# Attention of a hybrid layer taken step by step between the quarters of w_in's blocks

## The chip, the cores and the metric

One core of one Trainium2 chip runs the whole kernel. The metric is the device time of one execution in microseconds (us). The engines are named PE (TensorE), DVE (VectorE), ACT (ScalarE), POOL (GpSimd) and SP (SyncE, which here only issues DMAs).

## What is computed

One inference step of a two-layer backbone (DEPTH 2) for two groups of 128 tokens (g = 0 and 1), each 1024 wide, all in float32. A layer does, for h = the adaLN-modulated input:

```
gate_b, gate_c, u, q, k, v, g_conv, g_attn = split(h @ w_in)              # 1024 x 6656
y_conv = (gate_b * short_conv(gate_c * u)) @ w_conv_out
s1, s2 = q1 @ k1^T, q2 @ k2^T      (two halves of 64 of each of 8 heads)
p      = softmax(s1 / 8) - lam * softmax(s2 / 8)
o      = rms_norm(p @ v) * (1 - lam_init);  y_attn = o @ w_attn_out
x      = layer_norm(ALPHA * x + gate * ((sigmoid(g_conv) * y_conv + sigmoid(g_attn) * y_attn) @ w_out))
```

Group 1 has rotary positions on q and k, and 128 more cached keys and values. Behind it each layer has a channel mixer: a dense SwiGLU in layer 0, the top 2 of 8 SwiGLU experts in layer 1. The adaLN vectors are silu(c) @ ada_w, 24 blocks of 512 columns for both layers. Keys and values are outputs too.

## The kernel before

**Products in three passes.** A float32 weight block (1024 x 512 or 512 x 1024, 2 MB) is split into `w_hi` (ACT, `hi`, L535) and `w_lo` = raw - w_hi (DVE, `lo`, L816; a few blocks by POOL, `rests`, L441). PE multiplies with `mm3` (L1270 to L1272): hi*hi, lo*hi, hi*lo. A block is handled in four quarters (`PARTS`); `w_hi` and `w_lo` hold one buffer for each quarter, so the split of quarter t + 4 waits until PE has multiplied quarter t (`parts_free`). A quarter is 12 matmuls of 512 columns.

**Loads.** SP loads blocks into `raw`, a ring of three slots (`SLOTS`) of two halves each, in an order written out by hand. A half is 1 MB. A slot's half is loaded again once the block three places before it in `stream` is used up. The ada blocks stand in three lumps: 4 at the start, 12 behind `w_attn_out`'s first block of layer 0, 8 at the same place of layer 1 (`ADA_AT`).

**Order of a layer's first part.** 13 blocks of w_in (q, k, v, then gate_b, gate_c, u, then the four blocks of gates), whose results turn through three pairs of PSUM banks; the convolution's transposes (L1512) stand between the last of them. Then `w_conv_out`. Then attention: 16 heads (`JOBS`, 8 of group 0 and of group 1), in 20 steps of a software pipeline over PE, ACT and DVE. In step n, PE transposes q and k of head n (L1557 to L1560), multiplies the scores of head n - 1 (L1570) into one of two pairs of banks, takes ada halves (`ada_half`, L1465: 4 small products, 8 records in the trace; one half in each of 16 steps, and 8 more behind them in layer 0), transposes the probabilities of head n - 3 (L1583) and multiplies head n - 4 with v (L1591). DVE takes the maxima (L1176, L1178), scales and subtracts the two softmaxes (L1183 to L1187) and copies; ACT copies q and k (L734), takes exponentials with their sums (L742) and squares (L751). `ada_copy` (L578) empties the ada bank after each four blocks, `ada_turn` (L1476) transposes it. Behind attention come the transposes of the normed heads (L1533), `w_attn_out`, the gates' broadcast (L1360), `w_out` and the layer norm.

Each engine runs its program strictly in the order of its text, and waits on semaphores. POOL makes the normed x of the layer from `xhat` (`make_x`, L456 and L457), which lies where v's blocks will be written, so v's evacuation waits for it (`x_ok`).

Of the kernel before, what the change touches and what calls it, by code (L numbers as in the profile page):

```python
# [57 lines left out]
def program(nc, a, out):  # L58
    with ExitStack() as ctx:
# [37 lines left out]
        rsum = sb("rsum", [P, 2, 2])  # L97
# [21 lines left out]
        cv = sb("cv", [P, G, T])  # L119
        bank = [ctx.enter_context(nc.psum_tensor(f"bank{i}", [P, COL], F32)) for i in range(8)]  # L120
# [15 lines left out]
        att = flat[:, 0:2048]  # L136
# [3 lines left out]
        qkT = flat[:, 2048:2048 + 6 * T].rearrange("p (b k) -> p b k", b=2)  # L140
# [3 lines left out]
        rope_t = flat[:, 12288:13312]  # L144
# [15 lines left out]
        def s_bank(j, i):  # L160

            return bank[j % 2 + 6 * i]
# [7 lines left out]
        def head(b0, j):  # L170
# [31 lines left out]
            sem(n) for n in ("j_qk", "j_qkT", "j_s", "j_max", "j_exp", "j_p", "j_pT", "j_pTc", "j_o", "j_oc", "j_sq"))  # L202
        osd_ok, on_ok, oT_t, oT_hi, oT_ok = (sem(n) for n in ("osd_ok", "on_ok", "oT_t", "oT_hi", "oT_ok"))
# [22 lines left out]
        ADA_AT = [(0, 4), (IN_BLOCKS + 2, 12), (turn0[1] * SLOTS + IN_BLOCKS + 2, 8)]  # L226
        N_FIXED = (turn0[1] + Q_LAYER) * SLOTS
        stream = []
        for d in range(N_FIXED):
            for at, n in ADA_AT:  # L230
                if at == d:
                    stream += [("ada", sum(kind == "ada" for kind, _ in stream) + i) for i in range(n)]
            stream.append(("weights", d))
# [3 lines left out]
        def ring(q, s):  # L237

            if isinstance(q, int) and q * SLOTS + s < N_FIXED:
                i = place["weights", q * SLOTS + s]  # L240
                return i % SLOTS, i // SLOTS + 1
            return s, q + (RAW0 + 1)
# [10 lines left out]
        RUNS_IN = IN_BLOCKS // SLOTS  # L253
        RUNS_QKV = (B_GCONV - B_Q) // SLOTS
        ORDER_IN = list(range(B_Q, B_GCONV)) + list(range(B_GB, B_Q)) + list(range(B_GCONV, IN_BLOCKS))


        def halves(l, step):
            first = QUAD * 2 * (1 if l == 0 else 4)
            if step < JOBS:  # L260
                return [first + step]
            if l == 0:
                return [first + JOBS + 2 * (step - JOBS) + i for i in range(2)]
            return []

        TURN_AT = {9: 0, 17: 1}

        def quad_of(l, i):
            return i + (1 if l == 0 else 4)
# [9 lines left out]
        def _(sp):  # L279
            def free(i, half):  # L280

                if i >= SLOTS:
                    kind, n = stream[i - SLOTS]
                    if kind == "ada":
                        sp.wait_ge(ada_sum, n + 1)
                    else:
                        sp.wait_ge(lo_done, PARTS * n + 2 * half + 2)

            def load(q, s, half, shape, src):
                if isinstance(q, int) and q * SLOTS + s < N_FIXED:  # L290
                    free(place["weights", q * SLOTS + s], half)
                else:

                    sp.wait_ge(lo_done, (q - 1) * (PARTS * SLOTS) + (PARTS * s + 2 * half + 2))
                fill(ring(q, s)[0], half, shape, src)

            def fill(r, half, shape, src):
                n = shape[0] * shape[1]
                dst = raw[:, r, 2 * half * UNIT:2 * half * UNIT + n].rearrange("p (k n) -> p k n", n=shape[1])
                sp.dma_start(dst, src).then_inc(raw_in[r][half], 16)  # L300

            def conditioning(first, n):
                for k in range(first, first + n):
                    i, c0 = place["ada", k], k % ADA_BLOCKS * COL
                    for half in range(2):
                        free(i, half)
                        fill(i % SLOTS, half, (4, COL), a["ada_w"][k // ADA_BLOCKS][half * 4 * P:(half + 1) * 4 * P, :]
                             .rearrange("(k p) n -> p k n", p=P)[:, :, c0:c0 + COL])

            def columns(q, s, w, c0, n):  # L310

                for half in range(2):
                    load(q, s, half, (4, n), w[half * 4 * P:(half + 1) * 4 * P, :]
                         .rearrange("(k p) n -> p k n", p=P)[:, :, bass.ds(c0, n)])

            def rows(q, s, w, k0, k1):

                for half in range(2):
                    load(q, s, half, (k1 - k0, COL), w[k0 * P:k1 * P, half * COL:(half + 1) * COL]
                         .rearrange("(k p) n -> p k n", p=P))  # L320

            def expert(q, wg, wu, wd, others=None):
                for j in range(PER_EXPERT):
                    if others is not None and j == SLOTS:
                        others()
                    if j < 2 * CHUNKS:
                        columns(q + j // SLOTS, j % SLOTS, (wg, wu)[j % 2], j // 2 * COL, WIDE[j // 2])
                    else:
                        rows(q + j // SLOTS, j % SLOTS, wd, *DOWN[j - 2 * CHUNKS])
# [10 lines left out]
            conditioning(0, 4)  # L340
            for l in range(DEPTH):
                for pos, b in enumerate(ORDER_IN):
                    columns(turn0[l] + pos // SLOTS, pos % SLOTS, a["w_in"][l], b * COL, COL)
                q = turn0[l] + RUNS_IN
                rows(q, 1, a["w_conv_out"][l], 0, 4)
                rows(q, 2, a["w_attn_out"][l], 0, 4)
                conditioning(*((4, 12), (16, 8))[l])
                rows(q + 1, 0, a["w_attn_out"][l], 4, 8)
                rows(q + 1, 1, a["w_out"][l], 0, 4)
                rows(q + 1, 2, a["w_out"][l], 4, 8)  # L350
                q += 2
                if l == 0:
                    for e in range(DENSE_PARTS):
                        expert(q + e * Q_EXPERT, a["ffn_w_gate"][0][:, e * FF:(e + 1) * FF],
                               a["ffn_w_up"][0][:, e * FF:(e + 1) * FF], a["ffn_w_down"][0][e * FF:(e + 1) * FF, :])
                else:
                    def of(e):
                        return (a[n][0, bass.ds(e, 1)].rearrange("e d f -> (e d) f")
                                for n in ("moe_w_gate", "moe_w_up", "moe_w_down"))

                    def first_rows():
                        sp.wait_ge(x_sent, 16 * 2 * G)
                        x_load(0)
                        sp.wait_ge(gx_t, 1)
                        x_load(1)

                    def one(p, e):
                        def between():
                            y_store(p - 1, y_sent)
                            sp.wait_ge(gx_t, p + 1)  # L370
# [1326 lines left out]
```

## Time and profile before

| | |
|---|---|
| median of 3 runs | 1261.44 us (1261.29 to 1262.12) |
| the profiled execution | 1262.02 us, span 1260.2 us, mean granted clock 0.962 |
| w_in's blocks, layer 0 and 1 (from the first product) | 146.2 us and 157.2 us (with conv_out in layer 1) |
| attention, layer 0 and 1 | 63.7 us and 52.1 us |

The span is from the first to the last instruction. Busy time of PE counts matmuls whose ends are modelled: in a dense stretch they overlap, so that distances are better taken from start to start. The stretch from 44.7 to 190.9 us is w_in's 13 blocks of layer 0, 201.7 to 265.4 us its attention; 525.1 to 682.3 us is w_in and conv_out of layer 1, and 682.3 to 734.4 us its attention.

### The profile page before, as it was taken

The page shows a single profiled execution, that of the slowest core. Times are in us where ns is not written, and L with a number is a line of the kernel's source. Part 1 is how long each engine was busy: PE and PEld are TensorE (multiplying, and loading weights), DVE is VectorE, ACT ScalarE, POOL GpSimd, SP SyncE. Part 2 cuts the span into 40 slices and gives each one's busy share as a digit, 9 for nine tenths or more (in the row PEclk, how much of TensorE's full clock was granted, in tenths as well). Part 3 has the DMA queues.
Part 4 walks back from the last instruction along what each step waited for, and adds up shares of the span by engine and source line. Part 5 has one row for each costly group of instructions (what it writes and reads, how often), then busy time and mean ns, then how long its engine had stood idle before and what let it go on. Part 6 is the DMA issues. An engine that isn't in the chain of part 4 may idle for free.

```text
span 1260.2 us, 15915 instructions
## 1 busy us (share of the span) xinstructions
PE 1143.3 (91%) x5645; PEld 918.6 (73%) x5645; DVE 856.0 (68%) x1227; ACT 712.9 (57%) x1018; POOL 150.0 (12%) x140
## 2 busy tenths in 40 slices
PE   5699999889999999899999989649999999999980
PEld 1588885468789889788886478538888788788870
DVE  1574686635675455585676846539889889889965
ACT  1444455534644444444445644438888888888862
POOL 5040003000360000440003000340000000000001
PEclk9799999999999999999999989869999999999995
DMA  9777657985359746565656964069999999999952
GB/s 333 281 262 231 198 172 265 386 325 192 96 171 413 270 155 210 141 225 189 223 169 229 387 215 134 1 239 337 372 381 385 381 374 383 378 385 381 374 211 100
DMA packets 165849, 332.57 MB, mean 264 GB/s; under 512 B 6528, under 2 KB 27120, under 8 KB 165792
## 3 DMA queue, kind: packets, MB, share of 16 engines
q1 hardware_dynamic: 158288, 307.78, 69.6%
q0 software_dynamic: 7472, 24.03, 5.5%
q8 instruction: 36, 0.59, 0.2%
q14 instruction: 21, 0.17, 0.0%
q10 hardware_dynamic: 32, 0.01, 0.0%
HBM read 314.48 MB, written 17.30 MB: 263 GB/s over the span
## 4 chain that ended last, share of the span: by engine, by line
PE 79%; DVE 7%; DMA 5%; ACT 4%; issue 3%; POOL 0%; SPq 0%; ACTq 0%; DVEq 0%; POOLq 0%
PE bank L1270 24%; PE bank L1272 23%; PE bank L1271 23%; DMA raw<-in_ada_w 4%; PE bank L1465 2%; ACT w_hi L535 2%; PE bank L1360 1%; DVE xT_lo L851 1%; PE bank L1420 1%; DVE x L864 1%; DVE w_lo L816 1%; ACT xT_hi L558 1%; PE bank L1570 1%; PE bank L1409 1%; DVE st L821 1%
## 5 line engine op out<-in xcount | busy, mean ns | idle before, releaser
L816 DVE TENSOR_TENSOR w_lo<-raw,w_hi 128x1024 fp32r<-128x1024 f32 (+1 forms) x484 | 568.4, 1206 | 225.5 <-ACT w_hi L535 223.6
L535 ACT ACTIVATE w_hi<-raw 128x1024 fp32r<-128x1024 f32 (+1 forms) x504 | 500.2, 1008 | 360.4 <-PE bank L1272 360.1
L1270 PE MATMUL bank<-w_hi,xT_hi 128*128 128x512 f32 (+1 forms) x1056 | 407.9, 386 | 18.5 <-DVE w_lo L816 12.3
L1272 PE MATMUL bank<-w_lo,xT_hi 128*128 128x512 f32 (+1 forms) x1056 | 402.9, 382 | 0.0
L1271 PE MATMUL bank<-w_hi,xT_lo 128*128 128x512 f32 (+1 forms) x1056 | 402.7, 381 | 0.0
L1270 PEld LDWEIGHTS bank<-w_hi,xT_hi 128*128 128x128 f32 x1056 | 199.6, 189 | 60.1 <-issue 11.6
L1272 PEld LDWEIGHTS bank<-w_lo,xT_hi 128*128 128x128 f32 x1056 | 199.4, 189 | 35.0
L1271 PEld LDWEIGHTS bank<-w_hi,xT_lo 128*128 128x128 f32 x1056 | 199.7, 189 | 33.0
L1270 PE MATMUL bank<-w_hi,hT_hi 128*128 128x512 f32 x360 | 142.9, 397 | 3.7 <-issue 3.7
L1272 PE MATMUL bank<-w_lo,hT_hi 128*128 128x512 f32 x360 | 141.5, 393 | 0.0
L1271 PE MATMUL bank<-w_hi,hT_lo 128*128 128x512 f32 x360 | 141.3, 392 | 0.0
L441 POOL TENSOR_TENSOR w_lo<-raw,w_hi 128x1024 fp32r<-128x1024 f32 x20 | 50.7, 2555 | 404.0 <-ACT w_hi L535 404.0
L1270 PEld LDWEIGHTS bank<-w_hi,hT_hi 128*128 128x128 f32 x360 | 68.3, 190 | 17.5 <-issue 4.1
L1272 PEld LDWEIGHTS bank<-w_lo,hT_hi 128*128 128x128 f32 x360 | 68.1, 189 | 14.6
L1271 PEld LDWEIGHTS bank<-w_hi,hT_lo 128*128 128x128 f32 x360 | 68.4, 190 | 13.6
L1465 PE MATMUL bank<-raw,cond_st 128*32 128x512 f32 x384 | 57.0, 671 | 18.3 <-DMA raw<-in_ada_w 13.8
L506 POOL DMA_INDIRECT work<-y_rows,row_no x4 | 3.9, 968 | 389.9 <-DMA y_rows<-work 389.0
L1465 PEld LDWEIGHTS bank<-raw,cond_st 128*32 128x32 f32 x384 | 8.0, 113 | 40.6 <-DMA raw<-in_ada_w 27.9
L742 ACT ACTIVATE work<-bank,nmx 128x128 f32<-128x128 f32 (+1 forms) x64 | 26.4, 418 | 13.1 <-DVE nmx L1178 12.7
L751 ACT ACTIVATE cv<-work 128x128 f32<-128x128 f32 x32 | 9.9, 310 | 30.6 <-DVE work L1199 30.6
L456 POOL TENSOR_TENSOR x<-work 128x1024 f32<-128x1024 f32 x8 | 21.7, 2710 | 33.7 <-DVE work L910 26.6
L457 POOL TENSOR_TENSOR x<-x,work 128x1024 f32<-128x1024 f32 x8 | 24.3, 3035 | 0.6
(235 smaller groups left out, 886.4 us busy)
## 6 DMA issues: line engine op xcount, KB each, us to landing
raw<-in_w_in SPq DMA_DIRECT2D x52, 1024.0 KB, 5.1
raw<-in_ada_w SPq DMA_DIRECT2D x48, 1024.0 KB, 11.4
raw<-in_moe_w_gate SPq DMA_DIRECT2D x32, 1024.0 KB, 7.4
raw<-in_moe_w_up SPq DMA_DIRECT2D x32, 1024.0 KB, 8.2
raw<-in_moe_w_down SPq DMA_DIRECT2D x32, 1024.0 KB, 7.8
raw<-in_moe_w_gate SPq DMA_DIRECT2D x16, 768.0 KB, 8.8
raw<-in_moe_w_up SPq DMA_DIRECT2D x16, 768.0 KB, 7.5
raw<-in_moe_w_down SPq DMA_DIRECT2D x16, 768.0 KB, 7.7
```

Of the source, the lines that this page charges most:

```text
L441: pool.tensor_tensor(w_lo[:, unit, 0:n], raw[:, ring(q, s)[0], at:at + n], w_hi[:, unit, 0:n].bitcast(F32), ALU.subtract)\
L456: then(pool.tensor_tensor(x[:, g, :], xhat[:, g, :], ln_gb[n][:, 0, :], ALU.mult))
L457: then(pool.tensor_tensor(x[:, g, :], x[:, g, :], ln_gb[n][:, 1, :], ALU.add))
L535: nc.scalar.activation(w_hi[:, unit, 0:n], raw[:, r, at:at + n], ACT.Copy).then_inc(hi_done, 1)
L558: nc.scalar.activation(xT_hi[:, :, g, :], modulated[:, g, :, :], ACT.Copy).then_inc(mod_hi, 1)
L742: ins = nc.scalar.activation(e_buf[:, j % 2, i, 0:n], s_bank(j, i)[:, 0:n], ACT.Exp, bias=nmx[:, j % 2, i:i + 1], scale=SCALE, accum_out=e ...
L816: V.tensor_tensor(w_lo[:, unit, 0:n], raw[:, ring(q, s)[0], at:at + n], w_hi[:, unit, 0:n].bitcast(F32), ALU.subtract).then_inc(lo_done, 1)
L821: ins = V.bn_stats(st[:, g, half, :], x[:, g, half * COL:(half + 1) * COL])
L1270: pe.matmul(o, hi, wh, start=start, stop=False)
L1271: pe.matmul(o, lo, wh, start=False, stop=False)
L1272: return pe.matmul(o, hi, wl, start=False, stop=stop)
L1465: ins = pe.matmul(bank[3][32 * j:32 * j + 32, :], cond_st[:, k, at:at + 32], raw[:, i % SLOTS, k * COL:(k + 1) * COL], start=v == 0 and ha ...
```

## The change

The attention phase is gone as a phase. A clock of ticks is laid over w_in's blocks: tick t is quarter t % 4 of block t // 4 (52 ticks). Head j starts at tick 10 + 2j and its five PE pieces are put between the quarters: transposes of q and k at tick 10 + 2j ahead of the quarter and scores behind it, transposes of p at 13 + 2j, product with v at 14 + 2j. The blocks come in the order q, k, v, q, k, v, so that the first eight heads need only the first three. Ada halves follow quarters: three in four ticks in layer 0 (24 from tick 5 to 35), every second tick in layer 1 (16). On DVE and ACT each tick first does the softmax work that is due, then one quarter of the weight split (`lo`, `hi`), for the quarter three ahead of PE's. Rotations, conv chunks and gates have ticks of their own. The results of w_in turn through two pairs of banks (0, 1 and 6, 7); a head's two scores go to banks 4 and 2, bank 2 also takes the transposes of q and k, so the next head's transposes wait for this head's exponentials; p's transposes and o share bank 5; ada and the conv transposes bank 3. The scaling of p by the first softmax's sum is put off to the copy of o, which removes one DVE operation of each head. The ring of raw is one of six halves, each freed by itself; `stream` is sorted by the tick that needs each half. Two weight blocks that POOL split (the first of w_attn_out in each layer) go to DVE. Behind w_in come conv_out, with the heads' transposes inside it, then w_attn_out as before.

```diff
-        ADA_AT = [(0, 4), (IN_BLOCKS + 2, 12), (turn0[1] * SLOTS + IN_BLOCKS + 2, 8)]
+        TICKS = PARTS * IN_BLOCKS
+        STEP0 = 2 * PARTS + 2
+        LATE_GATE = 9
+        GCU_AT = PARTS * LATE_GATE
+        CONV_AT = [GCU_AT + 1 + 3 * c for c in range(KC)]
+        def job_at(tick, behind):
+            j = (tick - behind - STEP0) // 2
+            return j if (tick - behind - STEP0) % 2 == 0 and 0 <= j < JOBS else None
+        def half_at(l, tick):
+            if not PARTS < tick < 9 * PARTS:
+                return None
+            if l == 0:
+                return None if tick % PARTS == 0 else 2 * QUAD * quads(l)[0] + tick // PARTS * 3 - 3 + tick % PARTS - 1
+            return None if tick % 2 == 0 else 2 * QUAD * quads(l)[0] + (tick - PARTS) // 2
+        stream = [("ada", n // 2, n % 2) for n in range(2 * QUAD)]
+            needed = [(PARTS * (r - 1) + 2 * half + 1, 0, ("weights", turn0[l] * SLOTS + r, half))
+                      for r in range(Q_LAYER * SLOTS) for half in range(2)]
...
+        ORDER_IN = [B_Q, B_K, B_V, B_Q + 1, B_K + 1, B_V + 1] + list(range(B_GB, B_Q)) + list(range(B_GCONV, IN_BLOCKS))
...
 # SP
+            def free(i):
+                if i >= 2 * SLOTS:
+                    kind, n, half = stream[i - 2 * SLOTS]
...
 # ACT
+                for tick in range(1, TICKS + 1):
+                    pos, unit = divmod(tick - 1, PARTS)
+                    if job_at(tick, 0) is not None:
+                        qk_kept(job_at(tick, 0))
+                    if unit == PARTS - 1 and pos != LATE_GATE:
+                        evacuated(pos)
+                    hi(*slot(l, pos + 1), (unit,))
+                    if quad_done(l, tick - 1) is not None:
+                        ada_copy(quad_done(l, tick - 1))
+                    if job_at(tick, 1) is not None:
+                        exponentials(job_at(tick, 1))
+                    if job_at(tick, 5) is not None:
+                        squares(job_at(tick, 5))
+                    if tick == STEP0 + 2 * JOBS:
+                        evacuated(LATE_GATE)
...
 # DVE
+                    if job_at(tick, 1) is not None:
+                        maxima(job_at(tick, 1))
+                    if job_at(tick, 3) is not None:
+                        turned(job_at(tick, 3))
+                    if job_at(tick, 2) is not None:
+                        difference(job_at(tick, 2))
+                    if job_at(tick, 4) is not None:
+                        head_kept(job_at(tick, 4))
...
+                    if unit == PARTS - 1 and ORDER_IN[pos] < B_GCONV:
+                        evacuated(pos)
+                    lo(*slot(l, pos + 1), (unit,))
...
+                    if conv_at(tick - 1) is not None:
+                        conv(conv_at(tick - 1))
...
 # PE
+                def qk_turned(j):
...
+                    if j >= 1:
+                        pe.wait_ge(j_exp, JOBS * l + j)
...
+                    for unit in range(PARTS):
+                        tick = PARTS * pos + unit
+                        if job_at(tick, 0) is not None:
+                            qk_turned(job_at(tick, 0))
+                        if job_at(tick, 4) is not None:
+                            valued(job_at(tick, 4))
+                        if job_at(tick, 3) is not None:
+                            p_turned(job_at(tick, 3))
...
+                        columns(*slot(l, pos), (unit,), outs, COL)
+                        if job_at(tick, 0) is not None:
...
+                            scored(job_at(tick, 0))
+                        if half_at(l, tick) is not None:
+                            ada_half(half_at(l, tick))
+                        if conv_at(tick) is not None:
+                            conv_transposes(conv_at(tick))
```

## Rows read from the trace of the kernel before

**Rows 1.** The page: busy time of the engines, and the chain that ended last.

```profile
PE 1143.3 (91%) x5645; PEld 918.6 (73%) x5645; DVE 856.0 (68%) x1227; ACT 712.9 (57%) x1018; POOL 150.0 (12%) x140
...
PE 79%; DVE 7%; DMA 5%; ACT 4%; issue 3%; POOL 0%; SPq 0%; ACTq 0%; DVEq 0%; POOLq 0%
```

**Rows 2.** Stretches: w_in blocks and attention of layer 0, then of layer 1.

```profile
44.70:190.90 146.20, 146.16 (x641) 120.90 (x642) 98.43 (x119) 65.10 (x73) 18.10 (x12) 0.98 0.63 212
...
201.70:265.40 63.70, 52.65 (x394) 23.89 (x392) 42.98 (x155) 31.67 (x121) 4.59 (x4) 0.97 1.01 370
...
525.10:682.30 157.20, 155.63 (x696) 128.52 (x697) 102.31 (x126) 74.50 (x86) 27.22 (x18) 1.00 0.61 195
682.30:734.40 52.10, 44.44 (x330) 23.44 (x328) 42.70 (x155) 31.32 (x120) 4.59 (x4) 0.96 1.01 366
```

**Rows 3.** Timeline of PE, attention of layer 0, one step. Columns: start, length, instruction.

```profile
212.77 1.06 PE L1465 MATMUL bank<-raw,cond_st 128*32 128x512 f32 x8
213.76 0.33 PE L1583 MATMUL bank<-ident,work 128*128 128x128 f32 x1
...
215.20 1.06 PE L1465 MATMUL bank<-raw,cond_st 128*32 128x512 f32 x8
```

**Rows 4.** The same timeline, later: each group of eight is half an ada block.

```profile
247.19 1.07 PE L1465 MATMUL bank<-raw,cond_st 128*32 128x512 f32 x8 [0.83 <-DMA raw<-in_ada_w]
249.87 1.06 PE L1465 MATMUL bank<-raw,cond_st 128*32 128x512 f32 x8 [1.61 <-DMA raw<-in_ada_w]
...
253.09 1.94 PE L1465 MATMUL bank<-raw,cond_st 128*32 128x512 f32 x8
```

**Rows 5.** Waits, attention of layer 0: who waited for whom, total, times, longest.

```profile
PE bank L1465 <- DMA raw<-in_ada_w: 5.7, 6, 1.6
...
PE bank L1465 <- ACT ada_rows L578: 2.7, 2, 1.5
```

**Rows 6.** Timeline of PE, first attn-out half block, layer 0.

```profile
265.40 0.47 PE L1270 MATMUL bank<-w_hi,hT_hi 128*128 128x512 f32 x1 [1.83 <-issue]
...
270.95 1.04 PE L1533 MATMUL bank<-ident,work 128*128 128x128 f32 x8
```

**Rows 7.** The same, layer 1.

```profile
734.37 0.76 PE L1270 MATMUL bank<-w_hi,hT_hi 128*128 128x512 f32 x1 [1.83 <-issue]
...
742.57 1.03 PE L1533 MATMUL bank<-ident,work 128*128 128x128 f32 x8
```

**Rows 8.** Timeline of PE: eight transposes between two quarters of a w_in block.

```profile
647.45 0.39 PE L1271 MATMUL bank<-w_hi,xT_lo 128*128 128x512 f32 x1
647.67 0.40 PE L1272 MATMUL bank<-w_lo,xT_hi 128*128 128x512 f32 x1
647.91 1.04 PE L1512 MATMUL bank<-ident,work 128*128 128x128 f32 x8
648.70 0.48 PE L1270 MATMUL bank<-w_hi,xT_hi 128*128 128x512 f32 x1
649.02 0.39 PE L1271 MATMUL bank<-w_hi,xT_lo 128*128 128x512 f32 x1
```

**Rows 9.** Groups of instructions by line: the two weight splits, one rotation product.

```profile
L816 DVE TENSOR_TENSOR w_lo<-raw,w_hi 128x1024 fp32r<-128x1024 f32 (+1 forms) x484 | 568.4, 1206 | 225.5 <-ACT w_hi L535 223.6
L535 ACT ACTIVATE w_hi<-raw 128x1024 fp32r<-128x1024 f32 (+1 forms) x504 | 500.2, 1008 | 360.4 <-PE bank L1272 360.1
...
L1033 DVE TENSOR_TENSOR work<-work,rope 128x256 f32<-128x256 f32 x8 | 3.3, 416 | 0.0
```

**Rows 10.** Timeline, one head: maxima and exponentials behind its scores.

```profile
212.88 0.76 DVE L1176 TENSOR_REDUCE mx<-bank 128x1 f32<-128x256 f32 x2 [0.38 <-PE bank L1570]
...
213.88 0.47 ACT L742 ACTIVATE work<-bank,nmx 128x256 f32<-128x256 f32 x1 [0.56 <-DVE nmx L1178]
...
214.70 0.20 ACT L742 ACTIVATION_READ_ACCUMULATOR work<-bank,nmx 128x1 f32 x1
```

**Rows 11.** Timeline of POOL, first w_in blocks of layer 0: last step of make_x.

```profile
79.55 3.27 POOL L457 TENSOR_TENSOR x<-x,work 128x1024 f32<-128x1024 f32 x1
```

More of the change, by code:

```diff
@@ L251, in cut, with slot @@
             return (0, first * n) if unit % 2 == 0 else (first * n, (chunks - first) * n)
[L253 to L269, printed above, removed]
+        ORDER_IN = [B_Q, B_K, B_V, B_Q + 1, B_K + 1, B_V + 1] + list(range(B_GB, B_Q)) + list(range(B_GCONV, IN_BLOCKS))
+        ROTATED = (0, 1, 3, 4)
+        def slot(l, pos):
+            return turn0[l] + pos // SLOTS, pos % SLOTS
         def multiplied(eng, q, s, unit=PARTS - 1):
@@ L279, in _ @@
         def _(sp):
-            def free(i, half):
-                if i >= SLOTS:
-                    kind, n = stream[i - SLOTS]
+            def free(i):
+                if i >= 2 * SLOTS:
+                    kind, n, half = stream[i - 2 * SLOTS]
                     if kind == "ada":
-                        sp.wait_ge(ada_sum, n + 1)
+                        sp.wait_ge(ada_sum, 2 * n + half + 1)
                     else:
                         sp.wait_ge(lo_done, PARTS * n + 2 * half + 2)
[L289 to L295, printed above, removed]
@@ L310, in columns, with fill @@
[L310 to L329, printed above, removed]
+            def fill(r, half, src, k, n):
+                dst = raw[:, r, 2 * half * UNIT:2 * half * UNIT + k * n].rearrange("p (k n) -> p k n", n=n)
+                sp.dma_start(dst, src).then_inc(raw_in[r][half], 16)
@@ new lines, in _, with of, first_rows @@
+            for i, (kind, n, half) in enumerate(stream):
+                free(i)
+                r, part, _ = seat(i)
+                fill(r, part, *source(kind, n, half))
+            q = turn0[1] + Q_LAYER
+            def of(e):
+                return tuple(a[n][0, bass.ds(e, 1)].rearrange("e d f -> (e d) f")
+                        for n in ("moe_w_gate", "moe_w_up", "moe_w_down"))
+            def first_rows():
+                sp.wait_ge(x_sent, 16 * 2 * G)
+                x_load(0)
+                sp.wait_ge(gx_t, 1)
+                x_load(1)
@@ new lines, in exponentials @@
+                def exponentials(j):
+                    n = keys(j)
+                    act.wait_ge(j_max, JOBS * l + j + 1)
+                    if j >= 2:
+                        act.wait_ge(j_p, JOBS * l + j - 1)
+                    for i in range(2):
+                        ins = nc.scalar.activation(e_buf[:, j % 2, i, 0:n], scores(i)[:, 0:n], ACT.Exp,
+                                                   bias=nmx[:, j % 2, i:i + 1], scale=SCALE,
+                                                   accum_out=esum[:, j % 2, i:i + 1])
+                    ins.then_inc(j_exp, 1)
@@ L1605, in _ @@
                 pe.wait_ge(oT_ok, 4 * l + 4)
                 gate_broadcast(2 * l)
[L1607 removed]
+                for unit in rows(q0 + 1, 0, ACC, hT_hi, hT_lo, 0, 4, False, True):
                     if unit == 2:
```

607 lines of the change are left out of this document (287 added, 320 removed).

## The prediction

> **What bounds the kernel now.** I read the page first: PE is busy for 91% of the span and holds 79% of the chain that ended last; DVE, DMA and ACT hold 16% of it together and "issue" 3% [rows 1]. So an edit is worth time only where PE stands still or runs at a low clock, and a wait of another engine is worth nothing unless PE ends up behind it. Then I cut the mixers of both layers into stretches [rows 2]. In w_in's blocks PE has no gap in layer 0 (146.16 of 146.20 us) and DVE is busy for 67% of the time. In attention PE is busy for only 52.65 of 63.70 us in layer 0 and for 44.44 of 52.10 us in layer 1, DMA is saturated (share 1.01, at 370 and 366 GB/s), and the granted clock falls to a mean of 0.97 and 0.96. The reader is to see two stretches of opposite kind side by side: one that has PE full and DMA at 0.63 or 0.61, one that has DMA full and PE with holes.
>
> The timeline of PE says what attention consists of. A full step takes 2.43 us from start to start, of which the ada half is 0.99 and the pieces of the head 1.44 [rows 3]. The steps stand without gaps there, so moving them gives nothing back by itself: they cost PE the same time wherever they stand. The holes are elsewhere. Late in layer 0's attention PE waits for each ada half, 2.68 us from one to the next where the work is 1.0 [rows 4]; the list of waits has 5.7 us on those loads and 2.7 us on the copy that empties the ada bank [rows 5]; and at the end the last heads trickle through four engines with nothing beside them. Behind such holes PE works at the low level of its clock: the half at 253.09 us takes 1.94 us instead of 1.07 [rows 4], and in layer 1 the first half of w_attn_out takes 8.20 us to the heads' transposes where layer 0 takes 5.55 [rows 6, 7], though both have 24 products.
>
> **Step 1, the holes removed.** Idle PE in attention: 63.70 - 52.65 = 11.05 us in layer 0, 52.10 - 44.44 = 7.66 us in layer 1 [rows 2]. Low clock: a mean of 0.97 over 63.7 us, with levels 1 and 0.5, is 3.8 us at 1.2 GHz, in which 1.9 us are lost when PE is busy; the same for 0.96 over 52.1 us gives 4.2 and 2.1 us, of which I take 1.2, since part of it lies in idle time already counted [rows 2]. The slow half of w_attn_out is 8.20 - 5.55 = 2.65 us more [rows 6, 7]. Sum: 11.05 + 7.66 + 1.9 + 1.2 + 2.65 = 24.5 us. The busy time counts modelled ends that reach some 0.15 us into each hole, so the true sum may be up to 2 us more.
>
> **Step 2, what PE still has to do.** All pieces remain: 32 heads, 40 ada halves, their turns, the same transposes. The number of PE instructions does not change, nor does any shape. New is where they stand: about 43 quarters of each layer now follow a group of small matmuls. The only such place in the trace of before is a group of eight transposes inside w_in [rows 8]: one full product follows another by 0.22 to 0.23 us, the first transpose comes 0.24 us behind the last product, the eight take 0.79 us (0.1 each, as in attention), and the second product behind them comes 0.32 us behind the first. So the way back to large products costs 0.09 us. 2 x 43 x 0.09 = 7.7 us. Against this, inside attention small groups met one another too; the change from transposes to scores and from an ada half to transposes cost about as much there, and one of these per head now lies under a large product: 32 x 0.09 = 2.9 us back. Net 5 us of cost. Bounds: 0, if a group costs only its work, and 10, if entering it costs as much as leaving it and nothing is returned.
>
> **Step 3, DVE and ACT beside PE.** Per two ticks PE has two quarters of 12 x 0.227 = 2.72 us, one head at 1.44 or less, and ada: 1.5 halves in layer 0, one in layer 1. That is 5.4 + 1.4 + 1.5 = 8.3 us and 7.9 us, and 6.9 us once ada has ended at tick 35. DVE has two splits of 1.21 [rows 9], maxima of 0.76 + 0.2 [rows 10], and, by the same kind of operation, about 1.9 for difference and copies and 0.35 for half an evacuation: 5.6 us. Rotations, six operations of 0.42 in a block [rows 9], add 1.3: 6.9, still below 7.9. Over the whole, DVE's 98.4 + 43.0 us of before [rows 2], plus the 4 x 1.21 us of a block taken over from POOL, minus 16 scalings, is 143 us in some 200. ACT has 65.1 + 31.7. So neither is the bound on the average; the convolution's ticks (38 to 47) alone come to about 7.3 us per two against 6.9. The split runs three quarters ahead, over 8 us, and covers that.
>
> **Step 4, the new wait.** Bank 2 holds a score and then the next head's transposes, so PE, at the head of every second tick, waits for the exponentials of the head before; queued behind that wait are the product with v and the quarter itself. Scores end, maxima start 0.11 us later, and the read of the second sum ends at 214.90, that is 2.13 us behind the end of the scores at 212.77 [rows 3, 10]. PE meanwhile has the quarter of the odd tick, 2.72 us, transposes of p at 0.2, and in most ticks one or two ada halves: 2.9 us of cover at the least, 3.9 in layer 1 up to tick 35, 4 to 5 in layer 0. ACT puts one split (1.01 [rows 9]) ahead of the exponentials; it starts when the quarter ends, before the scores, and is over when the maxima are. DVE can be late by a rotation (up to 1 us) only while ada gives 3.9 us of cover. Where ada is over, the cover is 0.8 us, and the convolution and the product of gate_c and u stand before the maxima of heads 13 and 14. I take 1 us of stall for each layer, 2 us in all; bounds 0 and 10.
>
> **Step 5, loads.** In layer 0 ticks 5 to 35 take 31 x 4.2 = 130 us of PE and 40 halves of 1.05 MB. At the pace of the loads in attention, 2.68 us each [rows 4], these are 107 us, and caches, keys, values and norm weights are two or three halves more. So the load fits, with a margin of some 15 us, and each half is asked for at least two ticks ahead. A sentence apart: the Trainium skill, DMA: Bandwidth & Descriptors, Specifications, puts the limit of one core's HBM traffic at about 358 GB/s, by which the same 42 MB would take an estimated 117 us and still fit; the trace does not agree, since attention's stretch has a mean of 370. Nothing in the sum comes from that figure. v's evacuation now comes at tick 12 instead of 20. POOL ended make_x at 82.8 us [rows 11]; block 2 ends at about 44.7 + 3 x 10.9 + 2.7 of low clock + 7 us of inserts, or 87 us. Even 5 us later the split already done would cover it. The joint behind w_in (heads' transposes in conv_out, DVE's extra split) has 5.4 us of PE work over it. I cost both at nothing; uncovered, either is 2 to 5 us, inside the bound of step 4. Start, dense mixer and experts are not touched.
>
> **The sum.** 1262.0 (the profiled execution) - 24.5 + 5 + 2 = 1244.5 us. The median of the runs lies 0.6 us below the profiled execution, so I forecast 1244 us.
>
> **Rivals.**
> (a) *One chain per head sets the pace.* If the way scores, maxima, exponentials takes longer than its cover, each head adds its excess, because the pipeline is only one head deep at bank 2. For it: the margin is only 0.8 us without ada, and DVE and ACT are in-order with splits in the queue. Against: 2.13 us in the trace at a comparable load. It decides at 17.5 / 32 = 0.55 us per head; at 1 us per head the result is 1244 + 32 = 1276 us, slower. Chance 8%.
> (b) *Loads set the pace in layer 0.* For it: three engines' traffic now falls together, and w_in's stretch shows a share of 0.63 for only 212 GB/s [rows 2], which in proportion is full at 337 GB/s, or 3.1 us per half: 124 us for 40, close to 130. With 3.4 us per half it starts to bind; at 3.6 us it is 144 - 130 = 14 us, or 1258 us, a gain that nearly vanishes. Chance 8%.
> (c) *Switching eats it.* If each group costs 0.09 us on both sides and again per semaphore, 0.3 us over 86 quarters is 25 us instead of 5: 1264 us, no change. In the trace waits already met cost nothing visible between quarters. Chance 3%.
> (d) The forecast, PE without holes: 81%.
>
> **How the numbers follow.** The likeliest case runs from 1234 (all of step 1 with its 2 us more, nothing paid) to 1258 (10 and a few us of stalls). (b) lies at the upper end. So 1234 to 1257 leaves out the upper parts of (a) and (c) and some of (b). 0.2% or 2.5 us is about what a measurement of this kernel can tell from no change: faster holds (d) and nearly all of (b), 0.90; within it 0.03; slower, (a) and half of (c), 0.07.
>
> **What the profile after would show.** Right: no stretch of 10 us with PE below 95% between the first product of w_in and the experts' routing, clock 1.00 there, DVE at 70 to 80% and DMA at 0.8 to 0.95 in layer 0's w_in; w_in's stretch longer by about 50 us in layer 0 and 42 in layer 1, attention's gone. Step 2: first products behind small groups 0.3 us apart. Wrong by (a): idle time before L-lines of the q transposes, released by the exponentials. By (b): waits of the ada products or of `w_hi` for DMA. By (c): PE "busy" and idle as forecast, yet the stretch longer.

## The result, and the profile after

The changed kernel takes 1244.89 us (median, 1243.76 to 1245.27), the kernel before on the same chip 1261.78 us: a ratio of 0.986 [0.9847, 0.9872], 16.9 us less. The profiled execution took 1244.88 us with a span of 1243.1. The forecast was 1244.

The page of the changed kernel, the lines that answer to [rows 1]:

```profile
PE 1142.6 (92%) x5645; PEld 906.7 (73%) x5645; DVE 853.1 (69%) x1203; ACT 714.9 (58%) x1022; POOL 127.9 (10%) x132
...
PE 84%; ACT 5%; DVE 4%; DMA 3%; issue 2%; POOL 0%; ACTq 0%; SPq 0%; DVEq 0%; POOLq 0%
```

PE does the same 5645 instructions and is busy as long as before. Of the chain it holds 84% instead of 79%; DVE, DMA and "issue" gave that up, and ACT gained one point, to which we come back.

Stretches of the changed kernel: mixer of layer 0 up to gate_c's broadcast, the ticks in it that hold heads and ada, the dense mixer, the mixer of layer 1, and the norm and router behind it. Columns: stretch, length, then busy us (instructions) of PE, PEld, DVE, ACT and POOL, granted clock, share of DMA, GB/s.

```profile
46.00:268.40 222.40, 222.40 (x1144) 159.37 (x1145) 147.46 (x272) 107.31 (x208) 18.30 (x14) 0.99 0.79 277
58.50:200.00 141.50, 141.50 (x766) 92.85 (x765) 90.79 (x182) 63.90 (x143) 17.22 (x12) 1.00 0.93 326
310.20:507.50 197.30, 193.83 (x925) 165.35 (x924) 112.66 (x118) 93.06 (x114) 30.35 (x26) 1.00 0.64 221
516.20:730.90 214.70, 213.17 (x1080) 156.84 (x1081) 151.12 (x275) 109.77 (x212) 22.22 (x17) 1.00 0.70 238
772.70:791.00 18.30, 8.85 (x41) 6.63 (x39) 11.06 (x20) 11.25 (x17) 7.26 (x4) 0.79 0.00 1
```

The same stretches of the kernel before, in the same order:

```profile
44.70:278.70 234.00, 222.47 (x1145) 164.52 (x1145) 146.93 (x281) 108.77 (x208) 28.69 (x18) 0.98 0.76 263
320.60:516.50 195.90, 193.70 (x926) 165.42 (x925) 112.00 (x116) 92.74 (x113) 31.38 (x26) 1.00 0.65 223
525.10:748.90 223.80, 214.57 (x1080) 163.76 (x1081) 151.01 (x287) 110.06 (x211) 31.81 (x21) 0.98 0.67 226
790.70:807.20 16.50, 8.50 (x41) 6.63 (x40) 10.04 (x18) 10.94 (x16) 7.96 (x3) 0.83 0.00 1
```

PE's busy time in layer 0's mixer stays at 222.4 us while the stretch shrinks from 234.00 to 222.40: the gap of 11.5 us is gone. In layer 1 the gap shrinks from 9.2 to 1.5 us. But two other stretches grew: the dense mixer by 1.4 us and the norm and router by 1.8 us, at a mean clock of 0.79. From the starts of the same PE instructions in both timelines, the whole span adds up (us):

| stretch | before | after | difference |
|---|---|---|---|
| up to the first w_in product | 44.7 | 46.0 | +1.2 |
| mixer, layer 0 | 275.8 | 264.2 | -11.6 |
| dense mixer | 195.9 | 197.3 | +1.4 |
| mixer, layer 1 | 274.2 | 265.2 | -9.0 |
| norm and router of layer 1 up to the routing's end | 42.4 | 44.6 | +2.2 |
| experts | 427.1 | 425.8 | -1.3 |
| span | 1260.2 | 1243.1 | -17.1 |

So the mixers gave 20.6 us and the rest took 3.5 back. The first row is chance: in the eleven other profiles of kernels with this change the first product of w_in stands at 43.8 to 45.4 us ten times and at 46.0 once (`sqrt_again`), though none of them changes anything ahead of it.

The waits of the changed kernel, layer 0 between 46 and 245 us, and layer 1 between 516 and 708 us (the last row). Columns: who waits for whom, total us, times, longest.

```profile
ACT qkT L713 <- PE bank L1550: 22.3, 8, 3.6
...
PE bank L1302 <- DVE w_lo L838: 9.8, 1, 9.8
ACT work L721 <- DVE nmx L1176: 8.3, 10, 1.4
...
PE bank L1302 <- DVE xT_lo L873: 2.5, 2, 1.3
```

In both stretches PE waits for no exponentials and no load. Its 9.8 us in layer 0 are the start of the kernel's first split, ahead of the first product; its 2.5 us in layer 1 stand at the norm, in front of the first products. The 5.7 and 2.7 us of [rows 5] are no longer there. What waits now is ACT, for PE, and that costs nothing.

### The profile page after: what moved, and what is told of

Same layout as the page of the kernel before. It is cut to its first block, busy times and chain, and to the rows that moved or that the text cites. A ratio compares the mean times of both kernels' runs of the same rounds, so it can differ in the third digit from the quotient of the medians.

```text
span 1243.1 us, 15877 instructions
## 1 busy us (share of the span) xinstructions
PE 1142.6 (92%) x5645; PEld 906.7 (73%) x5645; DVE 853.1 (69%) x1203; ACT 714.9 (58%) x1022; POOL 127.9 (10%) x132
## 4 chain that ended last, share of the span: by engine, by line
PE 84%; ACT 5%; DVE 4%; DMA 3%; issue 2%; POOL 0%; ACTq 0%; SPq 0%; DVEq 0%; POOLq 0%
PE bank L1302 24%; PE bank L1304 23%; PE bank L1303 23%; PE bank L1497 4%; ACT w_hi L556 2%; DMA raw<-in_ada_w 1%; PE bank L1560 1%; PE bank L1392 1%; PE bank L1578 1%; DVE xT_lo L873 1%; PE bank L1452 1%; PE bank L1568 1%; ACT work L574 1%; DVE w_lo L838 1%; ACT xT_hi L579 1%
## 5 line engine op out<-in xcount | busy, mean ns | idle before, releaser
L1302 PE MATMUL bank<-w_hi,xT_hi 128*128 128x512 f32 (+1 forms) x1056 | 414.3, 392 | 18.4 <-DVE w_lo L838 12.3
L464 POOL TENSOR_TENSOR w_lo<-raw,w_hi 128x1024 fp32r<-128x1024 f32 x12 | 29.8, 2492 | 294.2 <-ACT w_hi L556 294.2
L713 ACT ACTIVATE qkT<-bank 128x256 f32<-128x256 f32 (+1 forms) x32 | 14.0, 437 | 73.7 <-PE bank L1550 41.5
L1193 DVE TENSOR_SCALAR work<-bank,rsum 128x128 f32<-128x128 f32 x32 | 11.2, 351 | 45.9 <-PE bank L1578 45.9
L721 ACT ACTIVATE work<-bank,nmx 128x128 f32<-128x128 f32 (+1 forms) x64 | 26.3, 417 | 16.9 <-DVE nmx L1176 16.5
L1174 DVE TENSOR_REDUCE mx<-bank 128x1 f32<-128x128 f32 (+1 forms) x64 | 19.9, 352 | 14.7 <-PE bank L1560 13.4
```

What stands on the lines that cost most here:

```text
L464: pool.tensor_tensor(w_lo[:, unit, 0:n], raw[:, r, at:at + n], w_hi[:, unit, 0:n].bitcast(F32), ALU.subtract)\
L713: nc.scalar.activation(qkT[:, j % 2, 0:n], bank[QK][:, 0:n], ACT.Copy).then_inc(j_qkT, 1)
L721: ins = nc.scalar.activation(e_buf[:, j % 2, i, 0:n], scores(i)[:, 0:n], ACT.Exp, bias=nmx[:, j % 2, i:i + 1], scale=SCALE, accum_out=esum ...
L1174: ins = V.tensor_reduce(mx[:, y, i:i + 1], scores(i)[:, 0:n], AX_X, ALU.max)
L1302: pe.matmul(o, hi, wh, start=start, stop=False)
```

## The experiments

Four kernels ran beside each other (`sqrt_early`, `split_quarter`, `chain_1`, `chain_3`; before: 1262.07), then four more (`scale_p`, `gate_in_turn`, `ring_slots`, `ada_every_tick`; before: 1260.89), then three (`chain_behind`, `sqrt_again` and the changed kernel once more as a control; before: 1262.31). Between the three groups the ratios compare better than the times. The control, `after_again`, has the ratio 0.9846 [0.9832, 0.9859], 1243.14 us; its first product of w_in stands at 45.4 us, slightly above the range that was expected.

> The changed kernel itself, once more, beside the other runs on the same chip: 1244 to 1246 us, ratio 0.986 to 0.988. Its start (first product of w_in) should lie at 43.8 to 45.1 us, as in the other runs of its family, if the 45.97 us of its first profile was chance; at 46 if it was not.

**A wait in the layer norm that was not in the forecast.** ACT at the norm of layer 1, kernel before (start, length, instruction, what ended the wait):

```profile
789.15 0.28 ACT L539 ACTIVATE sd<-mv,eps_c 128x1 f32<-128x1 f32 x1
790.55 1.25 ACT L546 ACTIVATE work<-x,nmr,rstd 128x1024 f32<-128x1024 f32 x1 [1.12 <-DVE nmr L828]
```

The changed kernel, same place, ACT, DVE and POOL:

```profile
769.18 2.08 ACT L556 ACTIVATE w_hi<-raw 128x1024 fp32r<-128x1024 f32 x2 [6.58 <-PE bank L1304]
...
770.39 4.74 POOL L464 TENSOR_TENSOR w_lo<-raw,w_hi 128x1024 fp32r<-128x1024 f32 x2 [75.12 <-ACT w_hi L556]
...
771.28 1.28 ACT L560 ACT_TABLE_LOAD   x1
...
772.58 0.29 ACT L560 ACTIVATE sd<-mv,eps_c 128x1 f32<-128x1 f32 x1
...
773.10 2.05 DVE L850 SCALAR_TENSOR_TENSOR nmr<-mv,rstd 128x1 f32<-128x1 f32 x1
...
775.19 1.24 ACT L567 ACTIVATE work<-x,nmr,rstd 128x1024 f32<-128x1024 f32 x1 [2.32 <-DVE nmr L850]
```

Before, x is scaled 1.40 us after the square root starts; now 2.61 us, and the root itself is 1.28 us later because of a table load. In the kernel before the last function of ACT's mixer with a table of its own was the heads' Sqrt, so the norm's Sqrt found its table. Now some of w_in's gates (Sigmoid) come behind it. The edit touches ACT alone, where nothing waits for it:

```diff
                 heads_turned((2, 3))
+                nc.scalar.activation(sd[:, G:G + 1], eps_c[:, 0:1], ACT.Sqrt)
                 hi(q0 + 1, 0)
```

> The changed kernel with one more ACT instruction in each layer: a Sqrt of one column behind the copies of the turned heads, whose only use is to have Sqrt's table loaded there. In the changed kernel the table of Sqrt is loaded again (1.28 us) inside the layer norm behind w_out, because two Sigmoid gates now stand behind the heads' Sqrt. Theory (the load is on the path of the layer norm in both layers, and takes PE's cover away): 1.3 us less in layer 0 and 1.8 us less in layer 1, so 3 us less than the changed kernel, about 1241.8 us. Rival (the load is hidden, and the longer stretches behind w_out are chance of the clock): 1244.9, no change.

> The changed kernel with Sqrt's table loaded early, once more beside the changed kernel on the same chip: 3 to 4 us below it, 1241 to 1242 us, since the stretches behind the first norm of each layer were 1.4 and 2.2 us shorter in its first profile. If the gain was chance of the start (2.2 us earlier there), below 1.5 us.

`sqrt_early`: 1240.69 us, 0.9834 [0.9821, 0.9847]. `sqrt_again`, beside the control: 1240.43 us (1240.27 to 1241.93), 0.9827 [0.9813, 0.984], against the control's 1243.14 (1242.46 to 1245.06): 2.7 us less. The intervals of the two ratios touch, but no execution of the one reaches the other's range, and `sqrt_early` lies as low. The timeline of `sqrt_again`, the norm of layer 1:

```profile
769.52 0.28 ACT L560 ACTIVATE sd<-mv,eps_c 128x1 f32<-128x1 f32 x1
...
770.03 0.85 DVE L851 SCALAR_TENSOR_TENSOR nmr<-mv,rstd 128x1 f32<-128x1 f32 x1
...
770.92 1.25 ACT L567 ACTIVATE work<-x,nmr,rstd 128x1024 f32<-128x1024 f32 x1 [1.12 <-DVE nmr L851]
```

The distance of 1.40 us is back. By PE's starts the dense mixer takes 195.8 us against the control's 197.4, and from the norm of layer 1 to the end 467.5 against 470.4. This is the fastest version, below both kernels.

**The price of switching.** The ada half is put inside the quarter, behind the six products of its first k, so that it forms a small group by itself and does not share one with the head's transposes:

```diff
-                        columns(*slot(l, pos), (unit,), outs, COL)
...
+                        for k in range(2):
...
+                            if k == 0 and half_at(l, tick) is not None:
+                                ada_half(half_at(l, tick))
```

> The changed kernel, but each of the 40 ada halves stands in the middle of its quarter (behind 6 of its 12 products) instead of behind it. The work and the order of everything else are the same, there are only 40 more places where a small group is followed by large products. Theory (each way back to large products costs 0.1 us): 40 x 0.1 = 4 us more, 1248.9 us. Rival (the excess of the inserted stretch over its work comes from the heads' pieces themselves or from waits, not from the switch): 1244.9 us, within 0.5.

1248.35 us, 0.9891 [0.9876, 0.9906], some 4 to 6 us above the changed kernel and its control by the ratios. To the broadcast layer 0 takes 226.5 instead of 222.4 us (24 halves), layer 1 224.6 instead of 223.4 (16): 5.3 us, or 4.6 against the control's profile. These are not 40 more groups but 35: three halves of layer 0 and two of layer 1 stood alone between two quarters before the edit too, and the trace has 62 small groups instead of 41 in layer 0, 56 instead of 42 in layer 1. That makes 0.13 to 0.15 us each; layer 1, whose time to the broadcast is 223.4 us in the control as well, gives 0.09 by itself. PE's timeline of this kernel, a half and the product behind it, and the next:

```profile
103.09 1.06 PE L1497 MATMUL bank<-raw,cond_st 128*32 128x512 f32 x8
104.09 0.50 PE L1302 MATMUL bank<-w_hi,xT_hi 128*128 128x512 f32 x1
104.43 0.40 PE L1303 MATMUL bank<-w_hi,xT_lo 128*128 128x512 f32 x1
```

**The chain of one head.** Three or eight small copies (0.28 us each, to a buffer that nobody reads; nothing is left out) stand on ACT ahead of each head's exponentials and make the way from scores to exponentials longer by 0.92 and 2.49 us, all of it, since they stand behind the wait for the maxima (the diff is that of `chain_1`; `chain_3` has `range(8)`):

```diff
+                    for _ in range(3):
+                        then(nc.scalar.activation(junk[:, :], ident[:, 0:96], ACT.Copy))
                     for i in range(2):
```

> The changed kernel with three small ACT copies ahead of each head's exponentials, about 1 us per head, into a buffer that nothing reads. Theory of the forecast (the chain from scores to exponentials has cover of 0.8 us at the least and 2 to 3 us in most ticks, and 0.6 us of the added work lies beside the maxima): 0 to 1 us more, 1245 to 1246 us. Rival (the one-deep bank sets the pace of each head): 32 heads by 0.5 to 1 us, 16 to 32 us more.

> The same with eight such copies ahead of each head's exponentials, about 2.8 us per head. Theory of the forecast: the added way is about 2.2 us. It exceeds the cover by 1.4 us at the two or three heads of each layer that have no ada half beside them, by 0.4 us at most heads of layer 1, and at none or few of layer 0: 7 + 5 = 12 us more, 1257 us; PE should be seen waiting for the exponentials at the transposes of q. If ACT as a whole is full instead (the splits come late), PE waits for the split of w and the loss is of the order of 32 x 1 us.

`chain_1`: 1246.2 us, 0.9877 [0.9862, 0.9892]: not distinguishable from the changed kernel by the intervals. `chain_3`: 1268.54 us, 1.0043 [1.0026, 1.006], the only version slower than before, and 24 us above the changed kernel (23 by the ratios), twice the 12 us that were expected. Its waits of PE for the exponentials, layer 0 (46 to 260 us), then layer 1 (516 to 730 us):

```profile
PE bank L1552 <- ACT work L724: 7.5, 8, 1.9
...
PE bank L1552 <- ACT work L724: 10.8, 13, 1.9
```

The direct waits are 18.3 us, on transposes into bank 2, just where step 4 had put them. Two stretches hold more than their waits. Windows of `chain_3`, from one head's scores to the next, where ada has ended, in each layer:

```profile
199.00:212.70 13.70, 11.79 (x52) 9.05 (x51) 8.61 (x18) 6.07 (x17) 0.00 (x0) 0.77 0.66 225
676.80:690.50 13.70, 11.79 (x52) 9.05 (x51) 8.62 (x18) 6.07 (x17) 0.00 (x0) 0.77 0.64 212
```

The same head in the changed kernel:

```profile
658.00:666.60 8.60, 8.60 (x50) 6.97 (x49) 7.47 (x16) 3.81 (x9) 0.00 (x0) 1.00 0.71 245
```

and the wait itself, in `chain_3`'s timeline:

```profile
679.39 2.49 ACT L722 ACTIVATE junk<-ident 128x96 f32<-128x96 f32 x8 [1.37 <-DVE nmx L1179]
...
682.73 0.20 ACT L724 ACTIVATION_READ_ACCUMULATOR work<-bank,nmx 128x1 f32 x1
...
682.99 0.33 PE L1552 MATMUL bank<-ident,work 128*128 128x128 f32 x1 [1.91 <-ACT work L724]
```

One wait of 1.91 us makes this head 5.1 us longer, 13.7 against 8.6: behind the hole the clock is at its low level (0.77 in the mean of the stretch), and the remaining 3.2 us are work done at half speed. Two of these are 10 of the 24 us. The sum nearly closes: 18.3 us of waits and twice 3.2 us are 24.7. The profiled execution is the slowest of the six, and in it the two mixers, from the first product to the broadcast, are 27 to 28 us longer than in the profiles of the changed kernel and its control. The missing 3 us are at least in part waits that the list leaves out or counts short: at 27 of 30 places the transposes follow the exponentials' end by 0.05 to 0.21 us, so PE waits at nearly every head, while the list has 21 waits. How much that is was not separated. Under ada's cover a head takes hardly longer (scores at 117.71 and 127.02 us, 9.31 apart; in the changed kernel at 116.64 and 125.75, 9.11).

To tell the longer way from the mere load on ACT, the same eight copies go behind the exponentials' increment, where no one waits for them directly:

```diff
                     ins.then_inc(j_exp, 1)
+                    for _ in range(8):
+                        then(nc.scalar.activation(junk[:, :], ident[:, 0:96], ACT.Copy))
```

> The run with eight added copies per head again, but the copies stand behind the exponentials and their signal instead of ahead of them. ACT has the same work, in the same tick. Theory (the loss of 24 us came from the closed way of a head: exponentials late, so the difference and all of DVE's next tick late, so the next maxima late): the copies are now outside that way, 0 to 4 us more than the changed kernel. Rival (ACT is full with 2.5 us more per head, and everything on it is late): 15 us more or above, as with the copies ahead.

1247.97 us, 0.9884 [0.9869, 0.9899], 4.8 us above its control where `chain_3` is 24 above the changed kernel. Its waits of PE on the exponentials, layers 0 and 1 (one wait of 0.6 us in each for the copy that empties bank 5 comes to them):

```profile
PE bank L1552 <- ACT work L722: 0.9, 1, 0.9
...
PE bank L1552 <- ACT work L722: 1.1, 1, 1.1
```

The same work on ACT costs little off the way and much on it. That late exponentials also push DVE's splits and the next maxima back, so that the loss feeds itself, is not needed for the sum; no run excludes it.

**The loads.** First, one ada half in every tick in place of three in four, so that layer 0's halves are asked for faster:

```diff
-                return None if tick % PARTS == 0 else 2 * QUAD * quads(l)[0] + tick // PARTS * 3 - 3 + tick % PARTS - 1
+                return 2 * QUAD * quads(l)[0] + tick - PARTS - 1 if tick <= PARTS + 24 else None
```

> The changed kernel, but layer 0's 24 ada halves stand behind every quarter from tick 5 to 28, instead of three in four up to tick 35. The loads then ask for 6 halves in four ticks, 17.8 us, which is 2.97 us for each half against 2.68 us, the pace that the loads reached in the attention of before. Theory of the loads (rival b of the forecast: they bind at about 3.1 us per half in this mixture): PE waits for DMA at the ada products, 24 x 0.2 to 0.5 = 5 to 12 us more. Theory of the forecast (the full pace holds): 0 to 2 us more, from heads 9 to 13 that lose the ada half's cover.

1244.22 us, 0.9872 [0.9856, 0.9889]: no change. The stretch of its heads:

```profile
58.00:170.00 112.00, 112.00 (x619) 70.41 (x618) 70.79 (x138) 48.06 (x104) 17.21 (x12) 1.00 1.01 362
```

DMA is full here, at 362 GB/s, and PE is full too. Second, the ring frees a buffer only when both halves of the old pair are done with (the wait is for entry i-6 and for its partner), as whole blocks did:

```diff
-                if i >= 2 * SLOTS:
-                    kind, n, half = stream[i - 2 * SLOTS]
+                for before_i in (() if i < 2 * SLOTS else (i - 2 * SLOTS, (i - 2 * SLOTS) ^ 1)):
+                    kind, n, half = stream[before_i]
```

> The changed kernel with the freeing of the ring undone: a half is loaded again only when both halves of its slot are used up, as before the change; the order of the loads stays. Theory of the forecast (each half is asked for at least two ticks ahead, with a margin of some 15 us over layer 0): the loads come one or two ticks (4 to 8 us) later, which leaves them 4 to 8 us against 2.7 us for one and 5.4 for two in a row: 0 to 3 us more, and first waits for DMA at the ada products. Rival (loads are close to the bound in layer 0, where the share is 0.93): PE waits at each block, 8 blocks x 2 us or more, 16 us and up.

1245.93 us, 0.9881 [0.9865, 0.9898]: one wait of PE appears in its list of waits,

```profile
PE bank L1497 <- DMA raw<-in_ada_w: 1.6, 1, 1.6
```

and one of 0.6 us for the split in layer 1. The time is 1.0 us higher by the medians and 2.7 us by the ratios, whose intervals overlap; by PE's starts the two mixers take 2.7 to 3.4 us more up to the broadcast than in the profiles of the control and of the changed kernel. So the finer ring is worth some 1 to 3 us, which the times do not tell from nothing.

**DVE and ACT beside PE.** `scale_p` puts back the scaling that the change had taken away (both exponentials are multiplied by their sums' inverses before the difference, and the head's product is copied unscaled), one DVE operation more for each head:

```diff
+                    then(V.tensor_scalar(p_buf[:, y, 0:n], e_buf[:, y, 0, 0:n], rsum[:, r, 0:1], None, ALU.mult))
                     V.scalar_tensor_tensor(out=p_buf[:, y, 0:n], in0=e_buf[:, y, 1, 0:n], scalar=rsum[:, r, 1:2],
-                                           in1=e_buf[:, y, 0, 0:n], op0=ALU.mult, op1=ALU.add).then_inc(j_p, 1)
+                                           in1=p_buf[:, y, 0:n], op0=ALU.mult, op1=ALU.add).then_inc(j_p, 1)
```

`gate_in_turn` empties the late gate's banks in the order of the others instead of behind the last head:

```diff
-                        if unit == PARTS - 1 and pos != LATE_GATE:
+                        if unit == PARTS - 1:
...
-                    if tick == STEP0 + 2 * JOBS:
-                        evacuated(LATE_GATE)
```

> The changed kernel with one part undone: p is scaled by the first softmax's sum again by an operation of its own (0.29 to 0.35 us on DVE, ahead of the subtraction), and o is copied without a factor. Theory (DVE is not the bound and the head's way has cover): within 0.5 us of the changed kernel's 1244.9. Rival (DVE's order couples the heads, as the run with eight added copies suggests, and there is no cover left in the convolution's ticks): up to 32 x 0.4 = 13 us more.

> The changed kernel, but the first gate (block 9) is evacuated at its own tick 40, one tick ahead of the last head's exponentials, instead of at tick 42. Sigmoid's and Exp's tables are then loaded once more each in each layer, 2.6 us of ACT. Theory (no head waits behind the last exponentials, the splits are three quarters ahead): within 1 us of 1244.9. Rival (a table load in the head's way costs its length, as it does in the layer norm): 2.6 to 5 us more.

1243.6 us, 0.9866 [0.985, 0.9882], and 1245.04 us, 0.9877 [0.9861, 0.9893]: neither is distinguishable from the changed kernel. With `scale_p` PE has no new wait; with `gate_in_turn` it waits once in each layer, 0.8 us, where the transposes of p stand behind DVE's copy of o.

## Why the prediction was right, and where it was not

The time is right (1244 against 1244.89), by a right mechanism and by two errors that nearly cancel: the mixers gave 3.1 us more than was forecast, and the rest, costed at nothing, took 3.5 back. That they cancel is luck.

**Step 1, 2 and 4 together** were -24.5 + 5 + 2 = -17.5 us; the mixers gave -20.6. *Step 1*, the holes: PE has no gap in layer 0's mixer (222.40 of 222.40 us) and 1.5 us in layer 1's, with a clock of 0.99 and 1.00. *Step 4* is mis-sized by its whole 2 us: no wait on the exponentials occurs. From the end of a head's exponentials to the next head's transposes the changed kernel has 0.5 and 0.65 us in the last two heads of each layer and 1.3 to 3.5 us in all others, so the smallest cover stands where the step had it and is a little smaller than its 0.8 us; what was missing is the delay that would have used it up. `chain_1` adds 0.92 us per head, and PE waits 0.6 us in each layer, in two places, at these two heads. The danger was real: with 2.49 us it is 24 us. Rival (a)'s account of excess per head is right in place and short in price, since it does not have the clock: its "each head adds its excess" gives no 5.1 us for a wait of 1.9.

*Step 2*, the way back from small groups, was taken at 0.09 us. Behind a group the second product stands 0.31 to 0.34 us behind the first instead of 0.23. PE's timeline of the changed kernel:

```profile
82.80 0.49 PE L1560 MATMUL bank<-qkT 64*128 64x128 f32 x4
83.22 1.06 PE L1497 MATMUL bank<-raw,cond_st 128*32 128x512 f32 x8
84.21 0.50 PE L1302 MATMUL bank<-w_hi,xT_hi 128*128 128x512 f32 x1
84.55 0.40 PE L1303 MATMUL bank<-w_hi,xT_lo 128*128 128x512 f32 x1
```

That is 0.11 us here. Over the 41 groups of layer 0 and 42 of layer 1 up to the broadcast (step 2 took 43) the second product stands 0.31 us behind the first in the median, which is 0.09 us each and 7.4 us in all, against 7.7 forecast; `split_quarter` gives 0.09 to 0.15 per added group. So the size was right. What the mixers paid in all is 24.5 - 20.6 = 3.9 us, or up to 6 if step 1 had its 2 us more. Step 4 took none of it, so it stands against step 2's net 5 us alone; how its 2.9 us of return and the sum of the holes share the rest is not settled.

Rival (c), 0.3 us per quarter, is out by the same rows: 0.09 to 0.15 us per group were seen.

**Step 3** (DVE and ACT are not the bound) holds: `scale_p` and `gate_in_turn` cost nothing. DVE's share was put at 70 to 80% and is 66%, 147.46 of 222.40 us to the broadcast and 131.6 of the 198.8 us of w_in's stretch. The forecast of 143 us in some 200 is thus 11 us too high.

**Step 5**, the loads fit: DMA is at 0.93 and 326 GB/s in the heads' ticks and PE waits for none. w_in's stretch became 198.8 us in layer 0, from the first product to w_conv_out's first at 244.8, where 146.2 + 50 had been said. Rival (b) is refuted by `ada_every_tick`: it asks for a half every 2.97 us, PE waits for none, and the mixed traffic went at 362 GB/s. The rival's 337 GB/s came from dividing 212 GB/s by a share of 0.63; share and rate are not quite proportional, since the same division gives 351 GB/s at the share of 0.93 and 358 at 1.01. The Trainium skill, DMA: Bandwidth & Descriptors, Specifications, has about 358 GB/s as the limit of one core's HBM traffic; the trace has 362 here, 1% above it, and 370 in attention before, 3% above it, so where they differ the trace decides. POOL's last step of make_x, which answers to [rows 11], comes earlier than before:

```profile
77.50 2.38 POOL L480 TENSOR_TENSOR x<-x,work 128x1024 f32<-128x1024 f32 x1
```

**The step that failed** is the sentence "Start, dense mixer and experts are not touched". The change moves Sigmoid behind the heads' Sqrt on ACT, and the norm of each layer pays for it: by `sqrt_again` 1.6 us in layer 0 and 2.9 us in layer 1, together 4.5 us by PE's starts in one execution each, 2.7 us by the medians of five. In layer 1 part of it is the clock, which is the level of one execution: a mean of 0.88 from 769.4 to 787.0 us of `sqrt_again`, against 0.79 in the norm and router of the changed kernel. The forecast listed what moved on PE, DVE and the queues, and never asked which table ACT is left with. The Trainium skill, ScalarE: Activation LUTs, What ACT_TABLE_LOAD costs, puts a switch at 1283 ns for the load and 1380 ns for a drain. The trace agrees on the load, 1.28 us; a drain of that length does not show, as the load begins 0.02 us after the end of ACT's split (769.18 + 2.08 = 771.26), and the root 0.02 us after the load's end. By that page an estimated 2.7 us would be lost, by the row 1.3. The measured scaling of x was late by 2.5 us in layer 1, but of that 1.2 us have another cause, in the last section.

Of what the prediction said would be seen, four things are there (clock 1.00, DMA 0.8 to 0.95, the longer w_in, first products 0.3 us apart); "PE never below 95% for 10 us" holds inside the mixers and the dense mixer, but not around the layer norms, where PE waits for the normed x (in stretches of 10 us down to 80% near 315 us, 72% near 515 us and 23% in layer 1's norm). The kernel before has the like waits there; the forecast did not except them.

## What to carry to other kernels

A stage in which loads are the limit and one in which TensorE is can be laid over each other, and what it gives can be read ahead: the idle time and the low clock of the one stage, less about 0.1 us for each new group of small products, as long as no chain through other engines is delayed by more than its cover (0.5 us at the least here; 0.92 us of added delay at each head cost 0.6 us of waiting in a layer, and nothing that the times could tell). Past that point PE waits, and a wait long enough to bring the clock down costs more than its length. When work is moved on ScalarE, list the functions in their new order as well as the times: a table that the old order left in place may be gone where something waits for it, and one dummy activation at an idle moment buys it back.

## What the runs showed of the hardware

- One wait of 1.9 us cost 5.1 us, since it put the work behind it at the low clock (3.2 us); twice in `chain_3`, in both layers alike. Shorter waits didn't: one of 1.6 us follows in each layer (at 218.34 and 696.14 us), behind which the granted clock stays at 1.00, and this stretch of the same kernel holds five, of 1.1 us at most, at 1.00.

```profile
590.00:650.00 60.00, 56.02 (x300) 37.89 (x300) 36.73 (x85) 42.85 (x123) 3.05 (x4) 1.00 0.75 258
```

- The small operation on DVE that makes nmr (128x1) takes 0.16 us where POOL does nothing:

```profile
1223.27 0.16 DVE L850 SCALAR_TENSOR_TENSOR nmr<-mv,rstd 128x1 f32<-128x1 f32 x1
```

In the norms behind both layers' mixers and behind the dense mixer, in both kernels and in `sqrt_again`, it ends 0.01 to 0.03 us behind the weight split that POOL has under way, and takes as long as that: 0.26 us at 320.75 us of the changed kernel, 0.85 before and in `sqrt_again`, 2.05 behind the table load (773.10 + 2.05 = 775.15 against 770.39 + 4.74 = 775.13 us, where two splits end). It reads two inputs from SBUF. The Trainium skill, GPSIMD Engine Reference, Specifications, names contention with DVE instructions that have two SBUF inputs; this case's rows agree, by the ends alone, as no run moved POOL's splits. So the load of 1.28 us was nearly doubled here: nmr came just after POOL had begun the second of its two splits, half of 4.74 us behind 770.39, and sat it out. That a later root would always pay so was not tried.
- A copy that ACT does between two calls of Exp brings no table load: the eight copies of `chain_3` ran 0.3 us apart with none, and in `sqrt_again` the splits between the early Sqrt and the norm's brought none. In the experts of the kernel before, though, seven loads stand in front of a split, which is a copy too; why was not examined.

```profile
L535 ACT ACT_TABLE_LOAD x7 | 9.0, 1283 | 0.1
```
